# First matmuls of three stages on unnormalised rows, and a reordered hand-over from Q projection to attention

## The reference

```
def rmsnorm(x, w):
    return x * rsqrt(mean(x * x, -1) + EPS) * w
hx = rmsnorm(x, norm_mix[i]) * (1.0 + sc1) + sh1
x = x + g1 * mixer(hx)
x = x + g2 * swiglu(rmsnorm(x, norm_ffn[i]) * (1.0 + sc2) + sh2, w_in, w_out)
```

## Time and profile before

| | us |
|---|---|
| median of 3 runs (1734.92 to 1735.91) | 1735.9 |
| profiled execution, device time | 1733.2 |
| its span, first to last instruction | 1730.4 |
| TensorE busy | 1652.7 |
| DVE busy | 694.9 |
| ACT busy | 617.4 |
| mean granted TensorE clock | 0.976 |

### The profile page before, as it was taken

The page is one execution under the profiler, slowest core; times in us unless marked ns, Lnnn a source line. Parts: engine busy times, 40 slices in busy tenths (PEclk is TensorE's granted clock), DMA queues, the critical chain, the costliest instruction groups (busy, mean ns, idle before and its releaser), DMA issues.

```text
span 1730.4 us, 23948 instructions
## 1 busy us (share of the span) xinstructions
PE 1652.7 (96%) x9804; PEld 1377.1 (80%) x9804; DVE 694.9 (40%) x995; ACT 617.4 (36%) x898; POOL 98.6 (6%) x95
## 2 busy tenths in 40 slices
PE   7999999999899999999999998869999899999998
PEld 5889988888688888888888887656758688887886
DVE  5414446443622222222222246667663533333334
ACT  5224466432423211222111224766662432222223
POOL 0000000000000000000000000025450000000003
PEclk8999999999899999999999998979999899999999
DMA  9233200023334434434334121200002232332332
GB/s 336 84 122 98 74 25 25 25 98 98 98 98 114 129 98 127 116 97 141 102 101 142 43 91 36 87 25 1 1 1 73 73 97 97 98 97 87 92 92 93
DMA packets 195291, 152.90 MB, mean 88 GB/s; under 512 B 6082, under 2 KB 193646, under 8 KB 195214
## 3 DMA queue, kind: packets, MB, share of 16 engines
q1 hardware_dynamic: 195214, 151.82, 29.0%
HBM read 149.71 MB, written 2.10 MB: 88 GB/s over the span
## 4 chain that ended last, share of the span: by engine, by line
PE 87%; DVE 5%; ACT 4%; DMA 1%; issue 1%; SPq 1%; DVEq 0%; ACTq 0%
PE ps L496 84%; PE ps L979 2%; DVE w_lo L1444 1%; DVE tmp L1482 1%; DVE h_lo L1491 1%; ACT w_hi L1053 1%; DMA ada_pre<-in_w_ada 1%; ACT q_sw L1339 1%; DMA w_raw<-in_ffn_w_out 0%; DVE xT L1509 0%; SPq L316 0%; DVE ssq L1456 0%; DMA w_raw<-in_ffn_w_in 0%; PE ps L759 0%; DVE q_st L1856 0%
## 5 line engine op out<-in xcount | busy, mean ns | idle before, releaser
L496 PE MATMUL ps<-h_hi,w_hi 128*128 128x512 f32 (+1 forms) x1408 | 429.5, 363 | 16.7 <-DVE h_lo L1491 8.4
L496 PE MATMUL ps<-h_lo,w_hi 128*128 128x512 f32 (+1 forms) x1408 | 418.6, 355 | 0.0
L496 PE MATMUL ps<-h_hi,w_lo 128*128 128x512 f32 (+1 forms) x1408 | 418.0, 355 | 0.0
L1444 DVE TENSOR_TENSOR w_lo<-w_raw,w_hi 128x2048 fp32r<-128x2048 f32 (+1 forms) x93 | 208.9, 2246 | 397.2 <-ACT w_hi L1053 397.0
L1053 ACT ACTIVATE w_hi<-w_raw 128x2048 fp32r<-128x2048 f32 (+1 forms) x93 | 174.7, 1878 | 418.5 <-DMA w_raw<-in_ffn_w_in 244.4
L496 PEld LDWEIGHTS ps<-h_hi,w_hi 128*128 128x128 f32 x1408 | 260.8, 191 | 66.5 <-issue 23.2
L496 PEld LDWEIGHTS ps<-h_lo,w_hi 128*128 128x128 f32 x1408 | 268.0, 190 | 37.8
L496 PEld LDWEIGHTS ps<-h_hi,w_lo 128*128 128x128 f32 x1408 | 267.6, 190 | 37.8
L496 PE MATMUL ps<-a_hi,w_hi 128*128 128x512 f32 (+1 forms) x528 | 159.7, 357 | 1.7 <-DVE w_lo L1444 1.6
L496 PE MATMUL ps<-a_hi,w_lo 128*128 128x512 f32 (+1 forms) x528 | 157.9, 353 | 0.0
L496 PE MATMUL ps<-a_lo,w_hi 128*128 128x512 f32 (+1 forms) x528 | 157.9, 353 | 0.0
(11 more groups left out here) (212 smaller groups left out, 1910.6 us busy)
## 6 DMA issues: line engine op xcount, KB each, us to landing
w_raw<-in_ffn_w_in SPq DMA_DIRECT2D x88, 512.0 KB, 5.6
ada_w<-in_w_ada SPq DMA_DIRECT2D x41, 1024.0 KB, 5.4
w_raw<-in_ffn_w_out SPq DMA_DIRECT2D x32, 512.0 KB, 5.9
w_raw<-in_gla_w_in SPq DMA_DIRECT2D x24, 512.0 KB, 4.9
ada_pre<-in_w_ada SPq DMA_DIRECT2D x7, 1024.0 KB, 11.6
w_raw<-in_ffn_w_out SPq DMA_DIRECT2D x16, 384.0 KB, 3.6
w_raw<-in_swa_w_qkv SPq DMA_DIRECT2D x10, 512.0 KB, 4.5
w_raw<-in_gla_w_o SPq DMA_DIRECT2D x8, 512.0 KB, 7.0
```

The lines of the kernel that those rows point to most:

```text
L496: return pe.matmul(o, w, r, start=start, stop=stop, skip_group_check=skip)
L1444: dve.tensor_tensor(w_lo[s][:, 0:kc, :], raw_of(n)[:, 0:kc, :], w_hi[s][:, 0:kc, :].bitcast(F32), ALU.subtract).then_inc(wlo_ok, 1)
```

## The change

**First slabs** (F0, KV0, F1). While the output slabs of the stage before run, ACT and DVE write the high and low halves of x times scale (`raw_high`, `raw_low`), chunk by chunk after the residual, without the norm. For F0 and KV0 they go to `h_hi` and `h_lo`; for F1 to `rs_hi`, `rs_lo`. TensorE's `first_slab` multiplies those. It takes the statistics before chunk 3 and the spread before chunk 4 (F1: 5), and ends with 48 matmuls with two moving columns, the shifts of latent and context, into bank 7. ACT copies the spread factor to SBUF (`rb`), DVE makes the first slab's result from PSUM times `rb` and adds the bias row `bz`. The other slabs of the stage still read the normalised h, which `normal` and `modulate` now make in two parts around that eviction: chunks 0 to 3, then 4 to 7. `modulate` waits for `kf_done`, since h takes the place of the raw halves. At the Q stage only latent tokens of h are made.

**Q to attention.** The swapped halves are made by DMAs from SBUF to SBUF, four of 32 partitions each (`swap_halves` on SP's queue, between the loads). Slabs Q0+1 to Q0+3 are loaded to `ada_w` instead of `w_raw`. These slabs run column block by column block (`by_chunk`), so that ACT can take the first chunk at half time; Q0+3 goes to banks 6 and 7. Chunk 7 of Q is rotated inside attention's first seven steps on DVE, ACT and a fourth buffer set. `scores` waits per head for `ql_ok`, and uses the other pair of banks. The splits of SO0 and SO0+1 move into attention's steps 20 to 23 and 40 to 43, a quarter each (`high_part`, `low_part`).

```diff
+        def first_slab(n, e, segs, turn=None):
+            s, b0 = n % 2, slab_banks(n)
...
+            for k in range(DC):
+                if k == 2 and turn is not None:
+                    unit_turn(turn)
+                if k == 3:
+                    if turn is not None:
+                        pe.wait_ge(mod_ok, turn + 2)
+                    statistics(m, tiles)
+                if k == 4 + int(len(segs) == 1):
+                    spread(m, tiles)
+                pe.wait_ge(rl_ok, 8 * e + k + 1)
...
+                last.then_inc(kf_done, 1)
+            pe.wait_ge(rbs_ok, e + 1)
+            pe.wait_ge(sh_ok, 2 * e + 2)
+            for ch in range(2):
+                blk = slice(ch * P, (ch + 1) * P)
+                for k in range(DC):
+                    for j, (w, r) in enumerate(((w_hi, sh_hi), (w_hi, sh_lo), (w_lo, sh_hi))):
+                        last = mm(bank(7, 2 * ch, 2), w[s][:, k, blk], r[:, k, :], k == 0 and j == 0,
+                                  k == DC - 1 and j == 2, skip=True)
+            last.then_inc(slab_done, 1)
...
+        def raw_low(e, ch, segs):
+            dve.wait_ge(amul_ok, AMUL_BASE + e)
+            dve.wait_ge(rh_ok, 8 * e + ch + 1)
+            for s in segs:
                 c_ = int(s == CTX)
+                last = dve.scalar_tensor_tensor(raw_lo(e, ch, s), xT[:, ch, s[0]:s[1]], amul[:, ch, c_:c_ + 1],
+                                                raw_hi(e, ch, s).bitcast(F32), ALU.mult, ALU.subtract)
+            last.then_inc(rl_ok, 1)
...
+            def first(n, sh):
+                s = n % 2
+                deviation(5 + 2 * l, D, a // P)
+                split(n + 1)
+                spread_out(5 + 2 * l, a)
+                modulate(2 * l + 1, 2 * l, segs, sh, 0, 4)
+                act.wait_ge(bz_ok, 2 * l + 1)
+                act.wait_ge(zg_ok, l + 1)
...
+                modulate(2 * l + 1, 2 * l, segs, sh, 4, 6)
+                split(n + 2)
+                modulate(2 * l + 1, 2 * l, segs, sh, 6, 8)
...
+        def swap_halves(done, src, dst, sw):
+            sp.wait_ge(y_ok, done)
+            for q in range(4):
+                o, r = 32 * q, 32 * (q ^ 1)
+                sp.dma_start(dst[o:o + 32, :], src[r:r + 32, :]).then_inc(sw, 16)
+        swap_halves(1, y_rot[:, LC:T], y_half, sw_in[0])
+        for f in range(DC):
+            if f in (0, 2):
+                load_slab(Q0 + 2 + f // 2, 0, cols(swa_w_qkv[0], (2 + f // 2) * 256))
+            swap_halves(f + 2, q_rot[sw_set(f)], q_sw[sw_set(f)], sw_in[sw_set(f)])
...
+        q_taken(Q0)
+        split(Q0 + 2)
+        turn_q(0)
+        turn_q(1)
+        low(0)
+        low(1)
+        turn_q(2)
+        q_taken(Q0 + 1)
+        split(Q0 + 3)
+        low(2)
+        turn_q(3)
+        low(3)
+        turn_q(4)
+        low(4)
+        q_taken(Q0 + 2)
+        turn_q(5)
+        low(5)
+        turn_q(6)
+        low(6)
...
+            if i // 4 in (5, 10):
+                low_part(SO0 + i // 20 - 1, i % 4)
```

More of the change, by code:

```diff
@@ L511, in slab @@
                 pe.wait_ge(out_free[s], n // 2 + i)
[L512 to L524, removed]
[L525 removed]
+            for chunks in ((0,), (1,)) if by_chunk else ((0, 1),):
+                for k in range(kc):
+                    if k in before:
+                        before[k]()
+                    if k == 2 and turns is not None:
+                        unit_turn(turns, 2 * i)
+                    if k_wait:
+                        k_wait(k)
+                    x_hi, x_lo = rhs(k)
+                    for ch in chunks:
+                        blk = slice(ch * P, (ch + 1) * P)
+                        for j, (w, r) in enumerate(((w_hi, x_hi), (w_hi, x_lo), (w_lo, x_hi))):
+                            for sg in segs:
+                                last = mm(seg(b0, ch, sg), w[s][:, k, blk], r(sg), start=(k == 0 and j == 0 and
+                                          not (sg == CTX and ch == 1)), stop=(k == kc - 1 and j == 2),
+                                          skip=(sg == CTX))
+                if chunks == (0,):
+                    last.then_inc(front_done, 1)
             last.then_inc(slab_done, 1)
@@ L883, in ffn @@
                 if lead:
-                    for e in range(2):
-                        slab(n + e, 0, h_in, segs, k_wait=h_wait(2 * l + 1, per) if e == 0 else None,
-                             turns=unit_of(n) if e and has_unit(n) else None)
-                        if has_unit(n):
-                            unit(unit_of(n) + e)
+                    first_slab(n, 2 * l, segs, turn=unit_of(n) - 1 if has_unit(n) else None)
+                    if has_unit(n):
+                        unit(unit_of(n))
+                    slab(n + 1, 0, h_in, segs, k_wait=h_wait(2 * l + 1, per),
+                         before={6: lambda: unit_turn(unit_of(F0))} if has_unit(n) else {})
+                    if has_unit(n):
+                        unit(unit_of(n) + 1)
                 m = n + 2 * lead
@@ L1281, in _ @@
             unit_row(unit_of(n))
-        deviation(5, D)
+            for ch in range(2):
+                raw_high("gla", 0, 2 * (n - GO0) + ch, BOTH)
         def ffn(l, n0, segs):
@@ L1414, in _ @@
                 over_sum(i - 1)
+            if i == 5:
+                high(7)
+            if i // 4 in (5, 10):
+                high_part(SO0 + i // 20 - 1, i % 4)
             if i >= 2:
@@ L1423, in _ @@
         for n in range(SO0, F1):
-            split(n + 1)
+            if n > SO0:
+                split(n + 1)
             for ch in range(2):
                 squares("swa", 2 * (n - SO0) + ch, LC)
-        deviation(7, D, 2)
+            for ch in range(2):
+                raw_high("swa", 2, 2 * (n - SO0) + ch, (LAT,))
         ffn(1, F1, (LAT,))
@@ L1922, in _ @@
         out_lo(7)
+        scale_rows(48 + 32, V_NFFN + 8)
         for n in range(SO0, F1):
-            split(n + 1)
+            if n > SO0:
+                split(n + 1)
             plain(n, "swa", 2 * (n - SO0), 48 + 16, (LAT,), False)
+            for ch in range(2):
+                raw_low(2, 2 * (n - SO0) + ch, (LAT,))
         ffn(1, 7, F1, (LAT,))
```

372 lines of the change are left out of this document (270 added, 102 removed).

## The result

The changed kernel takes 1713.0 us (median of 4 runs, 1711.4 to 1717.5), the kernel before 1735.4 (4 runs, 1733.4 to 1735.9): a ratio of 0.9876, 95% interval 0.9856 to 0.9895, 22.4 us. The forecast was 1715, with 1707 to 1728 as the range. The profiled execution of the changed kernel is the longest of its four: 1717.5 us, span 1715.8, so the two profiled executions differ by 15.7 us only and the medians by 22.4.

What follows compares the result with a forecast made beforehand. TensorE, busy 1652.7 of 1730.4 us, was taken as the bound, with gains only where it idles or runs at low clock. 5.4 + 8.0 + 4.0 + 6.3 - 3.0 = 20.7 us gave 1715 us, range 1707 to 1728.

Steps and rivals of the forecast that it cites:

- the likeliest case: Whole kernel: the forecast itself, 1715 us, with 1708 to 1720 as its own range and a chance of 0.60.
- The Q stage: End of K/V to first row maximum: 58.7 us against 70.04, 11.3 gained, with VectorE setting the pace after Q0+2 starts.
- I charge 1 us per edge, 3 in all: Three first-slab edges: charge for the clock falling in the two-column matmul bursts, with ends 0 and 12.1 us.
- the clock falls in every burst: Rival, three edges: low clock in each burst costs 12.1 us, gain 11.6, 1724 us; chance 0.17.
- wrong if a two-column matmul takes over 0.2 us: Bursts at the edges: one of three signs that would show the prediction wrong; 0.116 us per matmul was taken.
- The first FFN: Entry to the first FFN: second slab starts at 461.7 against 467.05, 5.4 us gained before the clock charge.
- K/V: Entry to the K/V slab: 25.4 us against 33.33, 8.0 us gained before the clock charge.
- The second FFN: Its entry: 4.0 us gained, not 6.0, as ACT is held by the split of the slab after next.
- A two-column matmul: Shift matmuls at each edge: 0.116 us each, 5.6 us for 48, with 3.2 and 10.9 us as ends.
- What comes back later: Attention steps: 1.5 us for chunk 7 of Q and 3.5 us for eight quarter splits, 5.0 in all.
- The slower rival: Q stage swaps: four pieces land one after another, 9.2 us per swap, attention 31 us later, 1746 us; slower side 0.07.
- The change doesn't do what it says: Rival, edges: TensorE still waits for 1/rms before chunk 4, costing under 2 us per edge; no chance of its own.

Runs made afterwards that it cites:

- the third experiment: Changed kernel with each edge's 48 two-column matmuls set one or two behind each dense matmul from chunk 4 on; 1704.6 us, ratio 0.9822 to the kernel before.
- The run with 32: Spread matmuls and spread chunk 7 together, plus shift halves side by side as four columns, so 32 short matmuls an edge replace 48; 1697.8 us, ratio 0.9771.
- the fourth experiment: Changed kernel with the Exp table loaded before attention and Q's chunk 7 halves taken one head at a time; 1704.1 us, ratio 0.9814 to the kernel before.
- the first experiment: The changed kernel run once more, unaltered, as base for the other runs; 1711.2 us, ratio 0.9857 to the kernel before.
- the two best edits: Changed kernel with spread two-column matmuls, and with spread chunk 7 plus early Exp table load; both together took 1701.7 us, ratio 0.9799 to the kernel before.

## Why the prediction was right, and where its terms were off

The time was right: 1713.0 against 1715, inside the likeliest case's own range. It was so with terms off in both directions, and with medians that differ by more than either pair of profiles (14.6 and 20.2 us), so that a miss of only 2 us is partly luck. The Q stage gave more than forecast, the clock took more than it was charged.

**The clock was under-priced.** "I charge 1 us per edge, 3 in all", out of 0 to 12.1. The rival "the clock falls in every burst" is what both profiles of the changed kernel show, at all three edges. Its 1724 us did not come, as the falls cost less than its 12.1 us (whose terms, 3 x 2.7 + 2 x 1.9, make 11.9) and other stretches gave more. Spreading the matmuls out regains 6.6 us, and removing them 8.4 us beyond their own time. Without a charge the sum was 23.7; with these it is 15 to 17, not 20.7. The row that pointed there was at hand, though it could not decide: at 440 us the clock had fallen after light matmuls, but between them TensorE had also stood idle, 2.4 and 0.8 us. I let the 1.39 us at 288.59 speak against it, a burst a quarter as long. By my own sign, "wrong if a two-column matmul takes over 0.2 us", the low clock brings it there (0.213); over a whole burst the mean was 0.13 to 0.17. The Trainium skill, TensorE: Matmul & The Clock Gate, section "What's actually happening", says that the low clock is the default and activity releases it; here the clock fell to 0.50 while the page of the profile counts TensorE as busy all the time, so what the profile calls busy is not enough to keep it.

**The first FFN** gave 1.1 and 2.8 us where 5.4 less 1 were forecast (here and below the two profiles of the changed kernel, each against the first profile of the kernel before). The order of work was as worked out: with the clock held, it gives 611.4 - 606.3 = 5.1 us in the third experiment. **K/V** gave 5.9 and 7.6 us against 8.0 less 1. **The second FFN** with what follows gave 3.6 and 3.5 us against 4.0 less 1; there were no waits for the slab after next, and the clock took instead what that hold-up had been charged.

**A two-column matmul** costs 0.111 us at full clock (0.116 taken), 0.213 at the low one. The run with 32 shows that two or four columns cost the same, so the price goes with the matmul and its 128x128 weight load, not with these columns.

**The Q stage** gave 13.8 and 14.4 us up to the first row maximum, against 11.3: 83.7 and 81.4 us after the first FFN's last slab, forecast 84. Within it the idle time before Q0+2 was 1.0 us and not 4, that before the exponentials 9.5 and not 7. The chain that I counted, VectorE's, is the one that sets it (busy 44.5 of 56.3 us); its four waits for ScalarE's high halves, counted 1.3 us each, took 0.7, which makes 2.4 us, as much as the stage came out shorter in the first profile.

**What comes back later** was forecast as 5.0 us and is 6.3, but in the wrong place. The eight quarter splits, charged 3.5 us, cost 0.15: the steps take 2.35 us with them as without, for 0.68 us fits into a step of 2.36 in which VectorE is busy 1.59. The wait for ScalarE's quarter of the same step, which I feared, did not show. Chunk 7, charged 1.5 us as "those steps run at the low clock, where DVE has gaps", and the late table load, not foreseen, cost 6.1 of the 6.3. The gaps exist, but only for pieces that fit into one, as the fourth experiment shows: in halves, it costs nothing. And the clock's part was no fixed price: without a fall the same piece cost 2.1 us.

**The slower rival** fell. The four pieces of a swap were issued 0.59 us apart and landed in 2.0 us each, so a swap took about 3 x 0.59 + 2.0 = 3.8 us and not 9.2. Two of the nine took 5.4 and 5.9 us, over the 5 us that I had named as a sign of being wrong; VectorE waited 1.9 us in all for them. The Trainium skill, DMA: Bandwidth & Descriptors, section "Rules for kernel authors", says that two transfers to disjoint partition halves serialize, as they share the same engines; for pieces of 64 KB no such cost shows here. "The change doesn't do what it says" fell too: TensorE waits nowhere for 1/rms. The low end of the range, described as no clock charge and a third of the loop costs, comes to 1709 and not 1707; nothing hangs on it.

Open is by how much the two best edits overlap in the medians, and what makes the clock fall at 362 us in some executions. The medians of before and changed differ by 22.4 and, beside the first experiment, 24.3 us, the two pairs of profiles by 14.6 and 20.2; the clock differs between executions by enough to cover that, but single stretches can't be read from runs without a profile. Of the 3.6 us after attention the third edge itself gives 3.9 (24.7 to 20.8), and the slab behind it takes 2.1 back at the low clock (13.1 against 11.0). Another 1.9 lie late in the second FFN, at 1586 us, where TensorE waits 1.6 us for a low half of weights before the change (0.9 in the second profile) and not after it; why was not traced.

## What to carry to other kernels

A TensorE that shows 100% busy can still be losing half its speed: read the granted clock beside the busy time, and put light matmuls between dense ones rather than behind them. Work that is moved into a tight loop is free as long as each piece fits into one step's slack, and costs a stall and then the clock where it doesn't, so cut it to the slack. In a queue that waits in order, a load that is put behind a wait inherits it: look at what each issue stands behind before moving one.

## What the runs showed of the hardware

- Matmuls of 2 columns on a full 128x128 weight tile follow each other at 0.111 us at the full clock and 0.213 at the low one; set singly between dense ones, they add as much (5.2 us for 46), and those of 4 columns no more (1.8 us saved by 16 fewer).
- Behind 48 such matmuls back to back the granted clock had fallen to 0.50 in all 18 bursts of six profiles, 17 times inside the burst (5.5 to 8.1 us long) and once right at its end (5.3 us). Spread between dense ones, it stayed at 1.00 at all nine edges of three profiles.
- Whether the clock falls behind a stall of TensorE in attention differed within one execution: a whole weight split cost 5.3 us with the fall (stall 2.8 us) and 2.7 without (2.5 us).
- An SBUF-to-SBUF piece of 64 KB landed in 2.0 us, right behind 1 MB of weights on the same queue in 4.1 to 4.8.
- The load of the Exp table took 1.28 us, and its place in time is not fixed: before the change it ran at 1145.4 us, ahead of the first maximum at 1148.5; after it, with one more wait ahead of the first Exp, it ran behind the maximum and stood in the path, until one small activation brought it forward (step 2 took 2.5 us in place of 3.8).
